# One modulation half per step of the dense lines, from a slot of its own, and fewer halves in the second mixers

## What is computed

```python
for l in range(DEPTH):                                     # first block, D = 1024
    mod_l = (silu_c @ w_mod[l] + b_mod[l])[:, None, :]     # w_mod[l]: 1024 x 6144
    mod_c = (silu_cc @ w_mod[l] + b_mod[l])[None, None, :]
    sh1_l, sc1_l, g1_l, sh2_l, sc2_l, g2_l = jnp.split(mod_l, N_MOD, axis=-1)
    h_l = rmsnorm(x_lat, norm_mix_pre[l]) * (1.0 + sc1_l) + sh1_l
    m_l, m_c = hybrid_mixer(h_l, h_c, ...)
    x_lat = x_lat + g1_l * rmsnorm(m_l, norm_mix_post[l])
    f_l = rmsnorm(x_lat, norm_ffn_pre[l]) * (1.0 + sc2_l) + sh2_l
    x_lat = x_lat + g2_l * rmsnorm(swiglu(f_l, w_gate[l], w_up[l], w_down[l]), norm_ffn_post[l])
# swiglu(h) = (silu(h @ w_gate) * (h @ w_up)) @ w_down,  D_FF = 2816
# second block: the same with c_act @ w_ada[layer] (6144 wide) and c_act @ w_kv_ada (2048 wide)
```

## Time and profile before

| | us |
|---|---|
| median of 3 runs | 3225.58 (3225.44 to 3231.82) |
| profiled execution | 3237.74 |
| its span | 3236.4 |
| TensorE (PE) busy | 2852.5, 88% |
| VectorE (DVE) busy | 2021.7, 62% |
| ScalarE (ACT) busy | 1444.9, 45% |
| mean DMA rate | 208 GB/s |

### The profile page before, as it was taken

How to read it: one execution, slowest core, us unless ns; L and a number is a source line. 1 busy time by engine, 2 the same in 40 slices (tenths; PEclk the granted TensorE clock), 3 DMA queues, 4 the chain that set the end, 5 groups by cost and what they waited for, 6 DMA issues and landing times.

```text
span 3236.4 us, 34071 instructions
## 1 busy us (share of the span) xinstructions
PE 2852.5 (88%) x13650; PEld 2231.5 (69%) x13650; DVE 2021.7 (62%) x2426; ACT 1444.9 (45%) x1589; POOL 119.5 (4%) x172
## 2 busy tenths in 40 slices
PE   5988899999788789987899767859999999999996
PEld 3765578888555457876678656647787878877874
DVE  3565456565454336546555444448888888888886
ACT  3322354354332124332433322436666666666664
POOL 3022000000002100000000000000000000000000
PEclk8988999999888879988799877969999999999998
DMA  6443445554545664533145330039999999999994
GB/s 236 170 147 114 173 150 175 173 182 156 183 169 206 248 234 160 174 114 130 51 152 176 116 129 30 8 124 345 330 347 340 344 342 335 348 341 325 348 335 176
DMA packets 411154, 674.33 MB, mean 208 GB/s; under 512 B 23046, under 2 KB 348806, under 8 KB 377712
## 3 DMA queue, kind: packets, MB, share of 16 engines
q1 hardware_dynamic: 404096, 660.17, 57.8%
q0 software_dynamic: 4912, 6.67, 0.8%
q10 hardware_dynamic: 1984, 5.26, 0.5%
HBM read 670.93 MB, written 1.10 MB: 208 GB/s over the span
## 4 chain that ended last, share of the span: by engine, by line
PE 72%; DVE 12%; DMA 8%; ACT 6%; issue 2%; SPq 0%; DVEq 0%; ACTq 0%; POOL 0%; POOLq 0%
PE psum L558 19%; PE psum L559 18%; PE psum L560 18%; PE psum L76 9%; DMA wslot<-in_moe_w_up 4%; DVE wslot_r L568 3%; PE psum L372 3%; DMA dslot<-in_w_ada 2%; PE psum L1888 1%; PE psum L1381 1%; PE psum L2731 1%; PE psum L2786 1%; PE psum L1516 1%; DVE few L76 1%; ACT whi_r L76 1%
## 5 line engine op out<-in xcount | busy, mean ns | idle before, releaser
L568 DVE TENSOR_TENSOR wslot_r<-wslot,whi_r 128x2048 fp32r<-128x2048 f32 (+1 forms) x120 | 269.5, 2256 | 172.7 <-ACT whi_r L76 172.5
L559 PE MATMUL psum<-wslot_r,arena_r 128*128 128x512 f32 x896 | 353.5, 394 | 0.0
L558 PE MATMUL psum<-whi_r,xhi_r 128*128 128x512 f32 (+1 forms) x752 | 300.2, 399 | 12.0 <-DVE wslot_r L568 10.8
L560 PE MATMUL psum<-whi_r,xlo_r 128*128 128x512 f32 (+1 forms) x752 | 292.6, 389 | 0.0
L559 PE MATMUL psum<-wslot_r,xhi_r 128*128 128x512 f32 (+1 forms) x736 | 288.5, 392 | 0.0
L76 ACT ACTIVATE whi_r<-wslot 128x2048 fp32r<-128x2048 f32 (+1 forms) x120 | 224.3, 1880 | 114.7 <-DMA wslot<-in_w_up 59.9
L568 DVE TENSOR_TENSOR wslot_r<-wslot,arena_r 128x2048 fp32r<-128x2048 f32 x112 | 256.1, 2286 | 23.2 <-ACT arena_r L2634 22.8
L568 DVE TENSOR_TENSOR dslot_r<-dslot,wide_r 128x2048 fp32r<-128x2048 f32 x112 | 256.2, 2287 | 15.2 <-ACT wide_r L2645 14.4
L2645 ACT ACTIVATE wide_r<-dslot 128x2048 fp32r<-128x2048 f32 x112 | 214.5, 1915 | 50.6 <-DMA dslot<-in_moe_w_down 49.8
L2634 ACT ACTIVATE arena_r<-wslot 128x2048 fp32r<-128x2048 f32 x112 | 214.3, 1914 | 26.2 <-DMA wslot<-in_moe_w_up 25.3
L558 PE MATMUL psum<-wide_r,work_r 128*128 128x512 f32 x448 | 191.6, 428 | 6.0 <-DVE dslot_r L568 6.0
(11 more groups left out here) (468 smaller groups left out, 5935.9 us busy)
## 6 DMA issues: line engine op xcount, KB each, us to landing
wslot<-in_moe_w_gate SPq DMA_DIRECT2D x224, 512.0 KB, 5.6
wslot<-in_moe_w_up SPq DMA_DIRECT2D x224, 512.0 KB, 7.0
dslot<-in_moe_w_down SPq DMA_DIRECT2D x112, 1024.0 KB, 8.7
dslot<-in_w_ada SPq DMA_DIRECT2D x48, 1024.0 KB, 4.8
dslot<-in_w_mod SPq DMA_DIRECT2D x44, 1024.0 KB, 4.8
wslot<-in_w_gate SPq DMA_DIRECT2D x66, 512.0 KB, 5.4
wslot<-in_w_up SPq DMA_DIRECT2D x66, 512.0 KB, 6.2
dslot<-in_w_down SPq DMA_DIRECT2D x33, 1024.0 KB, 4.9
```

The lines of the kernel that those rows point to most:

```text
L558: t.matmul(out_, hi, w_hi, start=start, stop=False)
L559: t.matmul(out_, hi, w_lo, start=False, stop=False)
L560: return t.matmul(out_, lo, w_hi, start=False, stop=stop)
L568: return v.tensor_tensor(one_pass(lo), src, one_pass(hi), ALU.subtract)
```

## The change

`Line.run` calls a new function `modulate(n)` in each step, ahead of `up(n, 1)` (in step 0 behind `split_h`): one step of the generator, with the next half fetched at once into a slot of its own, `line_slot`, 8 KB per partition where the second `ld_hi` buffer was. In the last step but one what is fetched is used up and the slot given back. The down weights are rounded into the other buffer alone (the line's last step uses the slot's place), so `high_d(n-1)` and `low_d(n-1)` move into step n behind `up(n, 0)`, and `high_d` waits for the down products of the step before its own. Bank 7 belongs to the modulations during a line: both `turn`s and `evacuated` use bank 6. In the second mixers `fill(3)` becomes `fill(2)` and `fill(1)`, and `joint_out(1)` calls `settle()`.

```diff
+        if own_slot[0]:
+            slot = own_slot[0]
+        elif n < FIRST and n % 4 >= 2:
...
+    line_slot = Slot(nc, "s_mod", at("mod_half", 18432, 2048))
...
+        def d_hi(self, n):
+            return ld_hi[1 if n == self.n - 1 else 0]
+
         def high_d(self, n):
-            self.high[n] = ac.put(a.activation, one_pass(ld_hi[n % 2][:]), d_slots[n % 2].ap[:], ACT.Copy,
-                                  after=[self.d_there[n], self.down_[n - 2] if n >= 2 else self.up_[0, 1]])
+            free = line_slot.reader if n == self.n - 1 else self.down_[n - 1] if n else self.up_[0, 1]
+            self.high[n] = ac.put(a.activation, one_pass(self.d_hi(n)[:]), d_slots[n % 2].ap[:], ACT.Copy,
+                                  after=[self.d_there[n], free])
...
         def turn(self, n, tt):
-            bk = bank_for_pe(6 + tt)
+            bk = bank_for_pe(6)
...
+            def modulate(n):
+
+                if n == 0:
+                    own_slot[0], line_slot.reader, allow_ahead[0] = line_slot, self.up_[0, 1], False
+                else:
+                    mod_step()
+                if n == end - 1:
+                    while slot_at:
+                        mod_step()
+                    own_slot[0], allow_ahead[0] = None, True
+                elif not slot_at and at_step[0]:
+                    look_ahead(ahead[0])
...
             for n in range(self.n):
                 self.up(n, 0)
+                if n:
+                    self.high_d(n - 1)
+                    self.low_d(n - 1)
                 self.high_w(n + 1, 0)
...
                 beside(n)
+                if n:
+                    modulate(n)
...
                 self.turn(n, 0)
-                self.high_d(n)
                 self.split_h(n, 0)
-                self.low_d(n)
+                if n == 0:
+                    modulate(0)
...
                 if p_ != start:
-                    fill(2 if l == 0 else 3)
+                    fill(2)
...
-            fill(3 if l == 1 else 1)
+            fill(1)
...
-        if l == 0:
-            settle()
-        else:
-            while at_step[0]:
-                mod_step()
+        settle()
...
-                      (6, 7), ready)
+                      (6, 6), ready)
```

More of the change, by code:

```diff
@@ L306, in build @@
     mod_tiles = [(job, j) for job in jobs for j in range(job[3])]
-    slot_at, ahead, allow_ahead, last_half = {}, [0], [True], [None]
+    slot_at, ahead, allow_ahead, last_half, own_slot = {}, [0], [True], [None], [None]
     FIRST, MB = 8, 7
@@ L312, in fetch_half @@
         (name, w, b, nt, first, m, gs), j = mod_tiles[n // KD]
-        if n < FIRST and n % 4 >= 2:
+        if own_slot[0]:
+            slot = own_slot[0]
+        elif n < FIRST and n % 4 >= 2:
             slot = w_slots[n % 2]
@@ L827, in low_w @@
                 self.w_low[n, half] = ve.put(low, raw, raw, hi, after=[self.high[n, half]])
+        def d_hi(self, n):
+            return ld_hi[1 if n == self.n - 1 else 0]
         def high_d(self, n):
-            self.high[n] = ac.put(a.activation, one_pass(ld_hi[n % 2][:]), d_slots[n % 2].ap[:], ACT.Copy,
-                                  after=[self.d_there[n], self.down_[n - 2] if n >= 2 else self.up_[0, 1]])
+            free = line_slot.reader if n == self.n - 1 else self.down_[n - 1] if n else self.up_[0, 1]
+            self.high[n] = ac.put(a.activation, one_pass(self.d_hi(n)[:]), d_slots[n % 2].ap[:], ACT.Copy,
+                                  after=[self.d_there[n], free])
         def low_d(self, n):
             raw = d_slots[n % 2].ap[:]
-            self.d_low[n] = ve.put(low, raw, raw, ld_hi[n % 2][:], after=[self.high[n]])
+            self.d_low[n] = ve.put(low, raw, raw, self.d_hi(n)[:], after=[self.high[n]])
         def up(self, n, tt):
@@ L867, in split_h @@
         def split_h(self, n, tt):
-            src = psum[:, 6 + tt, 0:256].rearrange("p (k q) -> p k q", k=2)
+            src = psum[:, 6, 0:256].rearrange("p (k q) -> p k q", k=2)
             hi, lo = (z[:, n % 2, :, tt * P:(tt + 1) * P] for z in (lhT, lhl))
@@ L871, in split_h @@
             self.h_split[n, tt] = ve.put(low, lo, src, hi, after=[rounded])
-            read_by(6 + tt, self.h_split[n, tt])
+            read_by(6, self.h_split[n, tt])
         def downs(self, n, tts):
@@ L885, in downs @@
                         cols = slice(k * D + h * 512, k * D + (h + 1) * 512)
[L886 removed]
+                        mm = products3(bk, lhT[:, n % 2, k, q], lhl[:, n % 2, k, q], self.d_hi(n)[:, cols], d_slots[n % 2].ap[:, cols],
                                        first and k == 0, last and k == 1)
```

## The result

The changed kernel takes **3190.95 us** in the median (3189.39 to 3191.38), the kernel before beside it on the same chip 3227.02: a ratio of 0.9885 with a 95% interval of 0.9868 to 0.9902, 36 us less. The forecast was 3195, its range 3167 to 3223. The profiled execution of the changed kernel took 3190.83 us, its span is 3189.5.

What follows compares the result with a forecast made beforehand. Second mixers were taken as bound by modulation-half transfers and a low clock, lines by TensorE with idle DMA. Terms -78 - 20 + 43.6 + 17.0 + 3 + 4 = -30.4 us, on the median 3225.6 giving 3195 us; range 3167 to 3223.

Steps and rivals of the forecast that it cites:

- Line 0: 22-step dense line: 18 added halves at 1.10 us and 2 tiles at 2.1, 24.0 us; stage forecast +30.8 us.
- the bank: Both halves' transposes sharing one bank in line 0 would cost +3 us, bounds 0 and 8.
- The first half's wait: Step 1 of each line: 4.2 us behind step 2's weights, plus 2.4 of half rate; 6.6 a line, 3.8 in line 0.
- the 4.8 us: Earlier trace, after a wait ending at 841.69: matmuls taken as at half rate until 846.51, costing 2.4 us.
- Lines 1 and 2: Later dense lines: added halves and a turned tile cost 10.9 and 8.7 us, plus 6.6 us each for the first wait.
- The loop: Second mixers' attention stretch would fall from 186.9 to 109 us: gain 78 us, bounds 65 and 89.
- the marks of the first mixers: Times in the first mixers' same loop with `fill(1)`, 49.3, 21.9 and 31.4 us, used to size the second mixers' loop.
- The check by another way: Attention gain of 78 us split as 38 us of halves and tiles, 29 of waits, 11 of clock.
- Rival 2: Half of the mixers' 48.4 us of DMA waits return as waits for other engines: -6, 3219 us; chance 0.12.
- Rival 3: Each of 27 halves leaving the mixers was paid at the lower clock: 24 us more gain, 3171 us; chance 0.11.
- The projections: Second mixers' projections: two transfer waits vanish and the chain starts 10.8 us earlier; gain 20 us, bounds 12 and 25.
- The queue order: One buffer of rounded down weights, `high_d(n-1)` ahead on ScalarE in the lines: 0 us, -2 to +8, with 1.8 us slack.

Runs made afterwards that it cites:

- the run whose loop took 108.0 us: The changed kernel with each line's first half asked for earlier and, in the other steps, the half multiplied ahead of the side work: 3178.74 us, ratio 0.9853.
- the two other old loops: The kernel before with the single buffer's new order and one shared bank (3239.28 us), and with the new order only (3224.26 us); fills unchanged.

## Why the prediction was right, step by step

**Line 0** came to +30.8 us as forecast, and that it did so to the tenth is luck. What doesn't belong to the halves, order, bank and tiles, costs 11.1 us by the run without halves (forecast 7.2): the order -3.6, the bank 11 where its bounds were 0 to 8, the tiles 3.5. The halves with the first one's wait cost 19.7 (forecast 23.6), for the two reasons read from that run: a wait at the bank that they cover, and matmuls that run faster with them. The first half's wait was 4.66 us (forecast 4.2). Behind it line 0 stays at the lower level until 458.35, and that costs 2.9 us, not 2.4:

```profile
452.05 1.94 PE L374 MATMUL psum<-mod_half,cs 128*32 128x512 f32 x8 [4.66 <-DMA mod_half<-in_w_mod]
...
457.93 0.62 PE L560 MATMUL psum<-whi_r,xhi_r 128*128 128x512 f32 x1
458.35 0.43 PE L561 MATMUL psum<-wslot_r,xhi_r 128*128 128x512 f32 x1
```

In lines 1 and 2 it costs 1.5: 0.9 in the half itself and 0.6 in the matmuls behind it. The step that was mis-sized there is the reading of the earlier trace rows: the 4.8 us were taken as work at half rate throughout, and as one price for all lines. A further wait lies within them, in the kernel before:

```profile
843.37 0.79 PE L558 MATMUL psum<-ld_hi_r,lhT_r 128*128 128x512 f32 x1 [0.98 <-DVE lhl_r L568]
```

So the slow work there cost some 1.7 us, 1.4 of them in the seven matmuls from 843.37 to 846.51, not 2.4.

**Lines 1 and 2** are the plain cases. Line 1: 9.6 for eight halves and 6.0 for the first one's wait and clock, by the run without them, and 1.3 for the tile and the rest, 16.9 together (forecast 17.5). Line 2: 7.2, 6.3 and 1.1, 14.6 (15.3). A half was put too low by 0.10 and the wait with its clock too high by 0.3 to 0.6. The step with the tile is 2.3 us longer than the others (19.41 against 17.09), close to the 2.1 of the forecast; something else in each line is 1 us shorter, as it was in the run with order and bank (1.6 and 0.3 us).

**The loop** is where the forecast was furthest off: 109 us by the marks of the first mixers, 101.0 measured, and in these are 4.0 us of two halves behind the last values, the loop's last and that of `settle()`, which the forecast had put behind the loop (so the output, forecast +4, came to +1). Marks of the changed kernel, last work of the loop and first behind it:

```profile
1099.62 3.26 PE L1406 MATMUL psum<-kvd,PTj 128*128 128x64 f32 x16 [1.01 <-DVE PTj L76]
1102.80 3.96 PE L374 MATMUL psum<-dslot,cs 128*32 128x512 f32 x16
1106.69 0.54 PE L76 MATMUL psum<-c_ident,wslot 128*128 128x128 f32 x2
```

From the first scores (1005.69) to the values of the third unit (1050.68) are 45.0 us, to those at the scan's end (1069.87) 19.2, to the last values (1099.62) 29.8, against 49.3, 21.9 and 31.4 from the earlier trace rows: the step that was mis-sized is taking the first mixers' marks as they were, 4.3, 2.7 and 1.6 us too much. These hold slower matmuls and longer waits, 10.8 us for `PTj` on VectorE with one of 6.8, where the changed loop has 4.1 with one of 3.1, at a granted clock of 0.88 instead of 0.92. How much of the 8.6 us is the marks and how much the execution isn't settled: the run whose loop took 108.0 us has the same 599 records, and there the last values come 100.5 us behind the first scores (1097.06), against 102.6 by the marks and 93.9 here. The gain of 86 in place of 78 us hangs on the execution of the kernel before as well; against the two other old loops it is 79 and 81. The windows and waits of that stretch in the kernel before:

```profile
199.06:338.43 139.37, 117.45 (x819) 82.81 (x819) 78.83 (x106) 39.07 (x94) 41.72 (x43) 0.88 0.39 133
...
PE psum L1381 <- DVE PTj L76: 10.8, 5, 6.8
```

The check by another way (38 us of work, 29 of waits, 11 of clock) holds in its kinds: of the 86 us, 37 go with the bytes alone, by the run with a quarter of them, and what remains is 48 us (both with the 186.9 of the kernel before), of which 26 halves and four tiles at 1.08 and 2.1 are 36.5. The rest is the waits for `stage` (7.4 us before, none after) and the clock. Rival 2 had half of the 48.4 us of transfer waits come back. By the rows 13 us did: TensorE's waits for other engines are 9.7 us more in the projections (26.0 against 16.3) and 3 more in the loop, and the forecast's chain and marks held as much already. What stands in their place in the changed loop are waits for `PTj` and `dec`, 12.2 us, and such waits were in the first mixers' marks already, as its "against" said; but in the projections one did come back, the 9.17 us for `stage` shown above. Rival 3 had 24 us more; the loop gave 8 beyond the sum.

**The projections** gave 20.8 (20). The two steps of the working held: both waits of the earlier trace rows are gone, and the transposes come at 131.9 us behind the first fetch of `w_in` instead of 151.8. That this is also the floor, and that the halves left there cost nothing, was not seen.

**The queue order** cost 0 (bounds -2 to 8) by the run of the order alone. The Trainium skill ("TensorE: Matmul & The Clock Gate", "Architectural detail") has the queues of ScalarE and VectorE strictly first in, first out; by that a late rounding could have held up all behind it. The trace agrees once, in an early step of line 0: a wait of 3.9 us where the earlier trace rows had 1.69, since VectorE's low part of the down weights (526.05, 2.29 us, order alone) now stands right ahead of the next one. The steady steps have the slack that was read from the earlier trace rows.

**Not foreseen**: the last attention is 4.6 us longer. It is 307.6 to 308.1 us in all six profiles of kernels with 15 halves in the loop, 305.4 and 305.5 in the two with 29, 303.2 to 305.6 in those that have the old fills. Laid side by side the two traces drift apart and back by 0.5 to 1.7 us at some fifteen places, mostly in matmuls that run at the lower level in one and the upper in the other. Why the drift has one sign is open.

**Forecast against measurement as a whole**: -30.4 was the sum, -36 the difference of medians. In the two profiles the loop and the output gave 8 and 3 more than forecast, the last attention took 5 of it back. Since the old loop differs by 7 us between profiles, the 8 is partly chance.

## What to carry to other kernels

The price of a filler piece depends on the stage and on how many are there already: in one loop the first fourteen beyond 16 cost 1.75 us each and the next dozen 4.5 to 5.1, as the waits for the 1 MB transfers grow and the granted clock goes down with them. So move out first what is past that knee, and put it where it fills another wait of TensorE (ahead of work that waits for a bank), one piece a step. Before more is taken out of a stage, ask what its floor is: in the projections, taking away six pieces gave 20.8 us and taking away ten more gave nothing. And profile a stage more than once before a few us of it are explained: the same loop took 101 and 108 us.

## What the runs showed of the hardware that I had not expected

**The granted clock differs between executions of one kernel.** Two executions of one kernel run the same 599 records of the attention loop, with 13.8 and 14.3 us of the same waits, at a clock of 0.84 and of 0.92. They part 30 us behind the first scores. The second execution there, then the first:

```profile
1026.40:1036.40 10.00, 8.61 (x69) 6.70 (x68) 6.28 (x8) 1.21 (x3) 8.30 (x7) 1.00 0.18 52
```

```profile
1026.50:1036.50 10.00, 8.61 (x45) 6.79 (x44) 4.54 (x6) 0.00 (x0) 5.68 (x5) 0.66 0.01 2
```

TensorE is busy 8.61 us of ten in both, once at 1.00 for 69 matmuls, once at 0.66 for 45. In the twenty microseconds ahead both have a clock of 1.00 and busy times of 10.00 and 8.77 us, with 64 or 65 and 67 matmuls. So one profile each doesn't compare this stage more closely than by some 7 us, before the change or after it.

**Less work can lower the clock.** With a quarter of the columns in the halves' matmuls and the same transfers, the loop's clock fell from 0.78 (0.83 in the best of the old loops) to 0.64. Of 31.6 us of busy time taken away (42 halves, 56.0 to 24.4) the stage became only 3 to 10 us shorter.

**The slow time behind a wait isn't set by the wait's length.** The changed kernel has the same wait of 4.66 us ahead of the same half in lines 0 and 1. In line 0 the lower level lasts 6.3 us from the half's start, in line 1 3.6, half and all; the earlier trace rows have 4.8 us after a wait of 4.14, with one more wait in them. It costs 2.9, 1.5 and some 1.7 us. One price of the clock for all would be wrong.

**The clock can fall with no wait ahead.** With the first half asked for earlier, TensorE has no idle time near the turned tile of line 1, and 3.1 us after the 32 small matmuls begin it runs for 3.4 us at the lower level (0.50).
